# A three-part residual block in fp32 on TensorE: the first norm taken token by token on ACT, and x turned in pairs of chunks

## What is computed

```
def rms_norm(x, g, eps=NORM_EPS):
    x32 = x.astype(jnp.float32)
    y = x32 * lax.rsqrt(jnp.mean(x32 * x32, axis=-1, keepdims=True) + eps)
    return (y * g.astype(jnp.float32)).astype(x.dtype)
...
h = rms_norm(x, norm_mix_pre_g[l])
proj = h @ w_in[l]
```

## Time and profile before

| | us |
|---|---|
| median of 3 runs (1989.51 to 1991.07) | 1990.86 |
| the profiled execution, its own time | 1988.77 |
| its span, first to last instruction | 1987.0 |
| PE busy | 1940.8 (98%) |
| DVE busy | 992.2 (50%) |
| ACT busy | 751.4 (38%) |
| POOL busy | 246.1 (12%) |

### The profile page before, as it was taken

One profiled execution on the slowest core, in us unless ns is written; L12 is line 12 of the kernel. 1 busy time (PEld: TensorE's weight loads), 2 busy tenths in 40 slices (PEclk: granted clock), 3 DMA queues, 4 the chain that ended last, 5 costly groups with the idle time before them and its releaser, 6 DMA issues.

```text
span 1987.0 us, 22614 instructions
## 1 busy us (share of the span) xinstructions
PE 1940.8 (98%) x9020; PEld 1576.9 (79%) x9020; DVE 992.2 (50%) x1488; ACT 751.4 (38%) x1110; POOL 246.1 (12%) x248
## 2 busy tenths in 40 slices
PE   8999999999999999999999999999899999999997
PEld 6777788878888887788888877877787788888886
DVE  6677534373333335643333466777654444333334
ACT  5344523453223224432322355555543343222233
POOL 5221001201011011110100131022010011011012
PEclk9999999999999999999999999999999999999998
DMA  5212223433333324233333222122231233333322
GB/s 163 85 54 64 64 85 95 117 96 96 100 100 97 96 80 122 85 96 97 100 100 96 85 85 64 54 64 64 75 96 54 85 96 96 96 97 98 101 80 58
DMA packets 343402, 175.71 MB, mean 88 GB/s; under 512 B 6305, under 2 KB 343298, under 8 KB 343298
## 3 DMA queue, kind: packets, MB, share of 16 engines
q1 hardware_dynamic: 343298, 174.27, 30.2%
HBM read 172.15 MB, written 2.10 MB: 88 GB/s over the span
## 4 chain that ended last, share of the span: by engine, by line
PE 91%; DVE 4%; ACT 2%; issue 1%; DMA 0%; SPq 0%; POOL 0%; DVEq 0%; ACTq 0%
PE ps L979 28%; PE ps L983 28%; PE ps L981 27%; PE ps L1039 1%; PE ps L1072 1%; PE ps L1019 1%; DVE WL L1403 1%; PE ps L1117 1%; PE ps L992 1%; PE ps L1135 1%; PE ps L1028 1%; PE ps L1009 1%; PE ps L1002 1%; DMA RAW<-in_w_in 0%; PE ps L1053 0%
## 5 line engine op out<-in xcount | busy, mean ns | idle before, releaser
L1403 DVE TENSOR_TENSOR WL<-RAW,WH 128x1024 fp32r<-128x1024 f32 (+2 forms) x336 | 400.8, 1195 | 690.3 <-ACT WH L1175 690.2
L979 PE MATMUL ps<-HH,WH 128*128 128x512 f32 x1728 | 689.2, 399 | 7.9 <-DVE TS L1436 7.9
L983 PE MATMUL ps<-HL,WH 128*128 128x512 f32 x1728 | 675.7, 391 | 1.9 <-DVE HL L1413 1.8
L981 PE MATMUL ps<-HH,WL 128*128 128x512 f32 x1728 | 674.9, 391 | 1.1 <-DVE WL L1403 1.1
L1175 ACT ACTIVATE WH<-RAW 128x1024 fp32r<-128x1024 f32 (+2 forms) x336 | 342.4, 1021 | 550.3 <-PE ps L983 542.4
L979 PEld LDWEIGHTS ps<-HH,WH 128*128 128x128 f32 x1728 | 325.4, 188 | 84.2 <-DVE TS L1436 9.1
L983 PEld LDWEIGHTS ps<-HL,WH 128*128 128x128 f32 x1728 | 325.4, 188 | 74.0 <-DVE HL L1413 5.3
L981 PEld LDWEIGHTS ps<-HH,WL 128*128 128x128 f32 x1728 | 325.6, 188 | 72.9 <-issue 5.3
L979 PE MATMUL ps<-GH,WH 128*128 128x512 f32 x720 | 281.7, 391 | 0.0
L983 PE MATMUL ps<-GL,WH 128*128 128x512 f32 x720 | 280.6, 390 | 0.0
L981 PE MATMUL ps<-GH,WL 128*128 128x512 f32 x720 | 280.2, 389 | 0.0
(11 more groups left out here) (181 smaller groups left out, 1448.2 us busy)
## 6 DMA issues: line engine op xcount, KB each, us to landing
RAW<-in_ffn_w_gu SPq DMA_DIRECT2D x88, 512.0 KB, 3.8
RAW<-in_w_in SPq DMA_DIRECT2D x68, 512.0 KB, 3.9
RAW<-in_ffn_w_down SPq DMA_DIRECT2D x32, 512.0 KB, 4.1
RAW<-in_w_gate SPq DMA_DIRECT2D x22, 512.0 KB, 3.8
RAW<-in_w_up SPq DMA_DIRECT2D x22, 512.0 KB, 3.8
RAW<-in_w_out SPq DMA_DIRECT2D x16, 512.0 KB, 4.2
RAW<-in_mem_w_kv SPq DMA_DIRECT2D x16, 512.0 KB, 3.9
RAW<-in_w_down SPq DMA_DIRECT2D x16, 512.0 KB, 4.2
```

What stands on the lines that cost most here:

```text
L979: e.matmul(bk, wh, xh, start=k == 0, stop=False)
L981: e.matmul(bk, wl, xh, start=False, stop=False)
L983: last = e.matmul(bk, wh, xl, start=False, stop=k == kt - 1)
L1403: e.tensor_tensor(m["WL"][:, s, 0:kt, :], m["RAW"][:, n % NRAW, 0:kt, :], m["WH"][:, s, 0:kt, :].bitcast(F32), ALU.subtract).then_inc(*sg. ...
```

## The change

The generator `turns` goes, and with it the squares of whole chunks, POOL's adds and `rstd` for the first norm. In its place `first_pair` writes the order of the first two projections out by hand:

- `turn_pair` turns two chunks (eight transposes, two copies) and feeds both (HH and HL of each), with no square in the feed.
- `square_pair` has ACT square x as it was loaded, with tokens on the partitions: for a pair of chunks four instructions of 128x256 (one for each block of 128 tokens), each also summing its row to one column of `XS`. The squares themselves go to two scratch tiles that nobody reads.
- `norm_sums`: DVE adds up four columns for each token block and scales them to a mean of 128x4; ACT takes Ln and Exp of it.
- `norm_spread`: DVE does the Newton step on 128x4, writes the factor onto the diagonal of four 128x128 blocks, and PE multiplies them with the matrix of 1/1024 (the blocks carry a factor of 1024), which puts each token's factor in every partition; DVE copies that to `R`.

The order in the list is now: turn 0 and 1, split 0, turn 2 and 3, squares 0, q with chunks 0 and 1, split 1, turn 4 and 5, squares 2, q with chunks 2 and 3, k with chunks 0 to 3, turn 6 and 7, squares 4, both with chunks 4 and 5, squares 6, `norm_sums`, split 2, both with chunks 6 and 7, `norm_spread`, the two `normed`, splits 3 and 4. The loads are issued as x 0, weight 0, x 2, weight 1, x 4, x 6, weights 2 and 3, the small ones; the loads of weights 4, 5 and 6 stand around split 2.

```
@@ -209,6 +208,9 @@
     def norm(self, gen):
         if gen not in self.held:
             self.held[gen] = True
+            if gen == 0:
+                self.first_norm()
+                return ("n", 0)
             self.rstd(("n", gen), None if gen in SUMMED else ("n", gen), ("acc_last", ("n", gen)), "onesD", 0)
         return ("n", gen)
 
...
@@ -474,20 +476,64 @@
 
 
 
-    def turns(self):
-        for c in range(KD):
-            self.bank(("tx", c))
-            self.step("turn_x", c)
-            if c % 2:
-                self.tiles.give(("x", c - 1), ("tx", c))
-                self.tiles.give(("x", c), ("tx", c))
-            self.banks.give(("tx", c), ("x", (0, c)))
-            if c:
-                self.feed(0, c - 1, 0, ())
-            if c < 2:
-                self.split_to(self.n_split + 1)
-            yield
-        self.feed(0, c, 0, ())
+    def turn_pair(self, c):
+        for a in range(2):
+            self.bank(("tx", c + a))
+            self.step("turn_x", c + a)
+            self.banks.give(("tx", c + a), ("x", (0, c + a)))
+        for a in range(2):
+            self.step("feed", 0, c + a, c + a, ())
+
+    def square_pair(self, c):
+        for a in range(2):
+            self.tiles.take(("xq", c, a))
+        self.step("square_x", c)
+        for a in range(2):
+            self.tiles.give(("xq", c, a), ("xq", c))
+        for a in range(2):
+            self.tiles.give(("x", c + a), ("tx", c + 1), ("xq", c))
+
+    def first_pair(self, ps):
+
+        banks = [self.bank(("pb", key)) for key, *_ in ps]
+        self.weights += [(name, 0, KD, c0) for _, name, c0, *_ in ps]
+        self.groups.append((0, 2, ("H", 0, 0), banks, T, KD))
+        def mm(which, *ks):
+            for i in which:
+                for k in ks:
+                    self.step("mm", 0, k, (i,))
+
+        self.turn_pair(0)
+        self.step("split", 0)
+        self.turn_pair(2)
+        self.square_pair(0)
+        mm((0,), 0, 1)
+        self.step("split", 1)
+        self.n_split = 2
+        self.turn_pair(4)
+        self.square_pair(2)
+        mm((0,), 2, 3)
+        mm((1,), 0, 1, 2, 3)
+        self.turn_pair(6)
+        self.square_pair(4)
+        mm((0, 1), 4, 5)
+        self.square_pair(6)
+        self.step("norm_sums")
+        self.split_to(3)
+        mm((0, 1), 6, 7)
+        done = [self.normed(0, p[0], b, ("mm", i), *p[3:]) for i, (p, b) in enumerate(zip(ps, banks))]
+        self.split_to(2 + NSPL)
+        return done
+
+    def first_norm(self):
+
+        key = ("n", 0)
+        self.bank(("stat", key))
+        self.tiles.take("diag")
+        self.tiles.take(("R", key))
+        self.step("norm_spread", key)
+        self.tiles.give("diag", ("stat", key))
+        self.banks.give(("stat", key), ("R", key))
 
     def memory_in(self):
         def load(c):
...
@@ -550,7 +596,7 @@
                     gate(*early[0])
                     return None
                 if u == 0 and i == 0:
-                    return self.hgroup(0, ps[0:2], lambda: next(turn, None))
+                    return self.first_pair(ps[0:2])
                 if u == 0:
                     more_consts()
                     return self.hgroup(0, ps[2:3])
...
@@ -844,14 +890,13 @@
             self.tiles.take(("x", c + 1))
             assert self.tiles.slot["x", c + 1] == self.tiles.slot["x", c] + 1
             self.step("load_x", c)
-            if self.total:
+            if self.total and c < 4:
                 self.dma()
+        for _ in range(2 if self.total else 0):
+            self.dma()
         self.tiles.take("small")
         self.step("small_loads")
-        turn = self.turns()
-        for _ in range(EARLY):
-            next(turn)
-        self.first_block(turn)
+        self.first_block()
         self.second_block()
 
 
...
@@ -965,10 +1012,10 @@
                 i = e.transpose(bk[:, (2 * a + j) * P:(2 * a + j + 1) * P], v[:, j, a * P:(a + 1) * P], ident)
         i.then_inc(*sg.inc("mt", c))
 
-    def mm(gid, k):
+    def mm(gid, k, which=None):
         n, cnt, xs, banks, cols, kt = plan.groups[gid]
         xh, xl = at.x_hi(xs, k, cols), at.x_lo(xs, k, cols)
-        for i in range(cnt):
+        for i in which or range(cnt):
             s = (n + i) % NSPL
             bk = at.bank(banks[i])[:, 0:cols]
             wh, wl = m["WH"][:, s, k, :], m["WL"][:, s, k, :]
...
@@ -991,6 +1038,12 @@
             wait_all(at.bank_free(("stat", key)))
         e.matmul(at.bank(("stat", key)), m["onesD"], at.tile((key, c)), start=c == 0, stop=c == KD - 1).then_inc(
             *(sg.inc("ssq", (key, c)) if c < KD - 1 else sg.inc("stat", key)))
+
+    def norm_spread(key):
+        g.wait_ge(*sg.at("ones", 0))
+        g.wait_ge(*sg.at("diag", 0))
+        wait_all(at.bank_free(("stat", key)))
+        e.matmul(at.bank(("stat", key)), m["onesD"], at.tile("diag"), start=True, stop=True).then_inc(*sg.inc("stat", key))
 
     def rstd(key, acc, ev, ones, eps, cols):
         if acc is None:
...
@@ -1179,6 +1232,24 @@
         g.wait_ge(*sg.at("gain", 0 if gen == 0 else 1))
         wait_all(free)
         e.activation(m["HH"][:, c, :], X[:, c, :], ACT.Copy, scale=G[:, gcol:gcol + 1]).then_inc(*sg.inc("xh", ("H", gen, c)))
+
+    def square_x(c):
+        v = at.x_pair(c)
+        g.wait_ge(*sg.at(f"d_x{c}", c))
+        for j in range(4):
+            h = slice(j % 2 * 256, j % 2 * 256 + 256)
+            wait_all(at.tile_free(("xq", c, j // 2)))
+            o = e.activation(at.tile(("xq", c, j // 2))[:, h], v[:, j, :], ACT.Square, accum_out=m["XS"][:, 4 * j + c // 2:4 * j + c // 2 + 1])
+        o.then_inc(*sg.inc("xq", c))
+
+    def norm_sums():
+        N = m["XN"]
+        explog()
+        g.wait_ge(*sg.at("xm", 0))
+        g.wait_ge(*sg.at("ones", 0))
+        e.activation(N[:, 4:8], N[:, 0:4], ACT.Ln, bias=m["eps"][:, 0:1], scale=4.0).then_inc(*sg.inc("rs"))
+        g.wait_ge(*sg.last("rs"))
+        e.activation(N[:, 4:8], N[:, 4:8], ACT.Exp, scale=-0.5).then_inc(*sg.inc("xr", 0))
 
     def square(acc, home, src, cols, ev):
         g.wait_ge(*sg.at(*ev))
...
@@ -1413,6 +1484,33 @@
         e.scalar_tensor_tensor(m["HL"][:, c, :], X[:, c, :], G[:, gcol:gcol + 1], m["HH"][:, c, :].bitcast(F32),
                                ALU.mult, ALU.subtract).then_inc(*sg.inc("xl", ("H", gen, c)))
 
+    def norm_sums():
+        N = m["XN"]
+        for c in range(0, KD, 2):
+            g.wait_ge(*sg.at("xq", c))
+        e.tensor_reduce(N[:, 8:12], m["XS"].rearrange("p (i c) -> p i c", c=4), AX.X, ALU.add).then_inc(*sg.inc("xn"))
+        g.wait_ge(*sg.last("xn"))
+        e.tensor_scalar(N[:, 0:4], N[:, 8:12], 1.0 / D, None, ALU.mult).then_inc(*sg.inc("xm", 0))
+
+    def norm_spread(key):
+        N, d = m["XN"], at.tile("diag").rearrange("p (i f) -> p i f", f=P)
+        g.wait_ge(*sg.at("xr", 0))
+        e.scalar_tensor_tensor(N[:, 8:12], N[:, 4:8], 4.0, N[:, 4:8], ALU.mult, ALU.mult).then_inc(*sg.inc("xn"))
+        g.wait_ge(*sg.at("xm", 0))
+        g.wait_ge(*sg.last("xn"))
+        e.scalar_tensor_tensor(N[:, 8:12], N[:, 0:4], 1e-6, N[:, 8:12], ALU.add, ALU.mult).then_inc(*sg.inc("xn"))
+        g.wait_ge(*sg.last("xn"))
+        e.scalar_tensor_tensor(N[:, 4:8], N[:, 8:12], 3.0, N[:, 4:8], ALU.subtract, ALU.mult, reverse0=True).then_inc(*sg.inc("xn"))
+        g.wait_ge(*sg.last("xn"))
+        g.wait_ge(*sg.at("ident", 0))
+        wait_all(at.tile_free("diag"))
+        for j in range(4):
+            o = e.tensor_scalar(d[:, j, :], m["ident"], N[:, 4 + j:5 + j], float(D), ALU.mult, ALU.mult)
+        o.then_inc(*sg.inc("diag", 0))
+        g.wait_ge(*sg.at("stat", key))
+        wait_all(at.tile_free(("R", key)))
+        e.tensor_copy(at.tile(("R", key)), at.bank(("stat", key))).then_inc(*sg.inc("R", key))
+
     def square_last(acc, c, cols):
         a, s = at.tile(acc)[:, 0:cols], at.tile((acc, c))[:, 0:cols]
         g.wait_ge(*sg.at("sq", (acc, c)))
```

More of the change, by code:

```diff
@@ L27 @@
 NEG = -1.0e30
-EARLY = 3
 SUMMED = (1, 2)
@@ L514, in memory_in, with first_block @@
         self.tiles.give(("R", "mem"), ("mr", 0))
-    def first_block(self, turn):
+    def first_block(self):
         early = [(br, mt) for mt in range(3) for br in range(2)]
@@ L880, in view, with x_pair @@
         return self.bank(src[0])[:, src[1] * 256:(src[1] + 1) * 256]
+    def x_pair(self, c):
+        i = self.plan.tiles.slot["x", c]
+        return self.mem["TS"][:, i:i + 2, :].rearrange("p a t -> p (a t)").rearrange("p (i f) -> p i f", f=2 * P)
     def tile_free(self, key):
@@ L947, in turn_x @@
     def turn_x(c):
-        i = plan.tiles.slot["x", c // 2 * 2]
-        v = m["TS"][:, i:i + 2, :].rearrange("p a t -> p (a t)").rearrange("p (i f) -> p i f", f=2 * P)
-        bk, f = at.bank(("tx", c)), (c % 2) * P
+        v, bk, f = at.x_pair(c // 2 * 2), at.bank(("tx", c)), (c % 2) * P
         g.wait_ge(*sg.at("ident", 0))
@@ L1144, in finish @@
         o.then_inc(*sg.inc("fin", 0))
```

(13 more changed lines are left out.)

## The result

Over ten runs of each in one session the changed kernel took 1995.62 us (1995.08 to 1997.01) and the kernel before 1989.79 us (1988.58 to 1991.13): 5.8 us more, a ratio of 1.0027 with a 95% interval of 1.0019 to 1.0036. The forecast was +4.4 us. All differences in this study are under 0.4% of the time. The profiled execution took 1995.08 us, span 1993.4, against 1988.77 and 1987.0.

The account below looks back on a forecast made before the run. TensorE, 91% of the last-ending chain, was taken as the bound, with v's start to watch. A 2.1 us wait plus 2.3 us of clock gave +4.4 on 1990.86, forecast 1995.3 us, range 1991.3 to 1998.6.

Parts of the forecast that it names:

- Start of the spread: TensorE's norm_spread matmul ahead of v: at 30.6 us against 28.51 for the old column sum, +2.1 us.
- the last, the diagonal: DVE after WL2: three small vector steps, 0.55 us, and four 128x128 scalings, 0.9 us, before norm_spread's matmul.
- step 3: DVE's WL1 beside POOL's bias multiplications, from 15.12 to 16.80 us: 1.684 us as today, against 1.22; X4 queued behind.
- One count: DVE's HL subtractions beside POOL's adds: about 0.5 us gained at each of five, 2.5 us if on the path.
- The clock: TensorE behind the 4.8 us gap before norm_spread: restarts at half clock, +2.3 us, bounds 0 and 2.5.
- Rival (a): TensorE's clock stays high through the gap before the spread: only +2.1 us, 1993.0 us; chance 0.12.
- The sum: Whole program: 2.1 for the wait plus 2.3 for the clock, +4.4 us, 1995.3 us.
- later on the shift stays whole: Behind the first stage: the next stop, a DVE chain at 54.66 us started by a TensorE result, moves along.
- (b): First stage: squares at 0.50 us, +1.2; first group at half level until 19 us, +2; 1998.5 us; chance 0.2.
- (c): ACT, 11 to 25 us: diagonal ready by 25.8, v starts at 26.7, -2.7 us, 1988.2 us; chance 0.06.
- (d): ACT or WL1 1 to 2 us faster, gap under 4 us, brief clock fall: about +2, 1992 us; chance 0.12.
- The edits at nothing: Reordered loads (weight 2 some 2 us later) and POOL's constants some 20 us earlier: priced at no cost.

Follow-up runs that it names:

- v_first_split2_early: Changed kernel with the spread's matmul, R copy and q/k products behind v's matmuls, and split 2 ahead of squares 4: 1987.13 us, 0.9985 of the kernel before.
- gap_filled: Changed kernel with 20 matmuls of 128x512 that nobody reads on TensorE ahead of the spread's wait: 1993.07 us, 1.0013 of the kernel before.
- changed_again: Changed kernel run once more, unedited, for a second profile: 1994.93 us, 1.0027 of the kernel before.
- split2_early: Changed kernel with only split 2 moved ahead of the squares of chunks 4 to 7, v still behind the spread: 1993.64 us, 1.0019 of the kernel before.
- squares6_twice: Changed kernel with the four squares of the last pair of chunks done a second time on ACT: 1996.22 us, 1.0035 of the kernel before.
- v_first: Changed kernel with the spread's matmul, R copy and q/k products behind v's matmuls, split 2 still late: 1992.40 us, 1.0010 of the kernel before.

## Why the prediction held, point by point

**The mechanism** was the one forecast: q and k end at 25.9 (forecast 25.8), TensorE idles (5.5 us against 4.8) for the chain from squares over Ln and Exp to WL2 and the diagonal, and comes back at the lower clock. v_first_split2_early takes the wait away and the clock's fall with it, gap_filled the fall alone, and each does what the sum says.

**Start of the spread, +2.1 forecast, +2.9 measured** (31.38 against 28.51; +2.5 in changed_again). Squares at 0.40 were right. The step that was mis-sized is the last, the diagonal: 0.55 + 0.9 us forecast, 29.27 to 31.27 measured, 2.0. The three small steps take up to 0.43 us from one to the next when they follow a large one, and the scalings 1.05. Ln was 0.25 late too. Against that, WL1 took 1.23 us beside POOL's bias work, not 1.68: my step 3 priced a contention that was not there, and X3, which waited for its transposes (11.44 for 11.18), had by then put the squares and WL1's start back by 0.35 us. The two errors cancelled, which is luck. One count was wrong as well: six subtractions, not five, ran beside POOL's adds.

**The clock, +2.3 forecast, 1.6 to 2.9 measured**: 1.6 in the first profile (4.5 less 2.9), 2.9 in changed_again (5.3 less 2.5). I took the size from the length of the gap, and the runs don't bear that out: 3.0 us behind the gap of 4.17 (split2_early), 2.9 behind 7.56 (squares6_twice), and the half level lasted longest, 6.6 us, behind the shortest wait, 2.35 us in v_first. That 2.3 lies inside is partly luck. The Trainium skill (TensorE: Matmul & The Clock Gate, HAM oscillation) says that a long enough wait makes the next group start cold; both profiles, split2_early and squares6_twice agree, and gap_filled shows the cure. Rival (a), a clock that stays high, fell here for gaps of 4.2 to 7.6 us and for the wait of 2.35.

**The sum, +4.4 against +5.8.** That the forecast time, 1995.3, is 0.3 us from the measured one is luck: it stood on a median of three runs for the kernel before, 1990.86, and over ten runs that kernel took 1989.79. The stage gave 4.5 and 5.3. In the first profile the rest came from the fall at 122 to 126 us, a term that I had not in the sum, though I had seen such falls behind waits of 2.6 us. The part "later on the shift stays whole" was right for the queue at 54.66, which now starts at 59.16, and missed that the clock need not repeat itself.

**Rivals.** (b), dear squares and a first group at the half level until 19 us, didn't happen: the squares took 0.405 us each, and the matmuls, 0.43 us apart at first as in the kernel before, were 0.23 apart from 14.5 us. (c), the norm that keeps up, fell for the change as it is. Its price for a v without a wait was right: -2.7 there, and in v_first_split2_early and its rerun -2.9 in the marked row and -3.1 and -2.9 in the time. (d) didn't happen. The edits at nothing held, save that the loads are not free in the old order.

## What to carry to other kernels

Take work off an engine that is not the bound only after asking what stands behind its result in the bounding engine's own queue: here a shorter first group ended in front of a matmul that waited for a longer norm. Put the step that nobody needs yet behind the next independent group (one moved step and one moved split were worth 8 us between two versions of the same arithmetic). Price a new idle stretch of TensorE twice, once for the wait and once for the matmuls behind it, and give the second price a range: here it was 1.6 to 3.0 us and did not follow the length of the gap.

## What the runs showed of the hardware

The granted clock also fell behind a stretch with no wait over 1 us: 0.51 through 122.9 to 126. In changed_again and before, with the same instructions and waits, it stayed at 1.00. Eight steps of 0.43 us for 0.23 cost 1.6 us, over a quarter of what this study set out to explain.

HL, with two SBUF inputs, took 1.25 to 1.50 us beside POOL's adds of two tiles in the kernel before, and 0.74 alone. Each of the six ended 0.54 to 0.55 us behind the end of the add that it met, early or late in it, as if it had waited for that end. One pair from the kernel before:

```profile
18.48 1.29 POOL L1751 TENSOR_TENSOR TS<-TS 128x512 f32<-128x512 f32 x1 [0.73 <-ACT TS L1186]
...
18.83 1.49 DVE L1413 SCALAR_TENSOR_TENSOR HL<-X,G,HH 128x512 fp32r<-128x512 f32 x1
```

Beside a POOL multiplication by a constant there was no single price. DVE's WL1 took 1.23 us, as alone, where it started 0.8 us into one (changed kernel, 15.47 in 14.66 to 18.06). A WL that started together with one took 1.68 us in the kernel before. What decides between them was not tested.
